# Index scores of a sparse-attention layer: two of eight heads weighted and summed on TensorE with diagonal matrices

## The reference, cut to what matters

```python
sc = jnp.einsum('bqhd,bsd->bqhs', qi, ki).astype(jnp.float32)              # 8 heads, 32 wide
idx_score = jnp.einsum('bqhs,bqh->bqs', jax.nn.relu(sc), wi.astype(jnp.float32))
idx_score = jnp.where(chunk_mask(q_pos, k_pos)[None], idx_score, -jnp.inf)
_, sel = lax.top_k(idx_score, topk)
```

## Time and profile before

| | |
|---|---|
| median of 3 runs | 3009.12 us (3008.86 to 3010.0) |
| the profiled execution, own time | 3013.24 us |
| its span, first to last instruction | 3011.5 us |
| mean granted TensorE clock over the span | 0.962 of full speed |
| busy: PE, DVE, ACT, POOL | 93%, 67%, 47%, 18% of the span |
| the index-score stage | 229.8 to 291.2 us, 61.4 us, 2% of the span |

### The profile page before, as it was taken

One profiled execution on the slowest core, in us unless ns is written; L12 is line 12 of the kernel. 1 busy time (PEld: TensorE's weight loads), 2 busy tenths in 40 slices (PEclk: granted clock), 3 DMA queues, 4 the chain that ended last, 5 costly groups with the idle time before them and its releaser, 6 DMA issues. The chain is left out here.

```text
span 3011.5 us, 49026 instructions
## 1 busy us (share of the span) xinstructions
PE 2801.6 (93%) x18237; PEld 2366.5 (79%) x18237; DVE 2022.9 (67%) x3648; ACT 1413.7 (47%) x2850; POOL 536.1 (18%) x410
## 2 busy tenths in 40 slices
PE   8986997999899999899899799999898999998998
PEld 6762564668899999778799567865688999998887
DVE  5447999865767776787631665139757777677777
ACT  5335996552444344433243455348724444444333
POOL 0000222420001110465000231000000111114641
PEclk9995999999999999999999799999999999999999
DMA  4111001022223332653411201120212333326432
GB/s 154 46 36 29 14 14 50 2 65 74 68 93 108 107 100 93 238 170 128 169 50 53 85 2 53 56 77 2 65 67 61 100 107 101 102 92 226 155 129 103
DMA packets 203118, 259.01 MB, mean 86 GB/s; under 512 B 27100, under 2 KB 132180, under 8 KB 202900
## 3 DMA queue, kind: packets, MB, share of 16 engines
q1 hardware_dynamic: 202900, 256.10, 25.9%
HBM read 177.90 MB, written 77.64 MB: 85 GB/s over the span
## 5 line engine op out<-in xcount | busy, mean ns | idle before, releaser
L247 PE MATMUL X<-up_th,high 128*128 128x272 f32 x1232 | 358.8, 291 | 12.4 <-DVE mixed_a_r L2377 4.8
L249 PE MATMUL X<-up_th,low_r 128*128 128x272 f32 x1232 | 357.4, 290 | 0.0
L247 PEld LDWEIGHTS X<-up_th,high 128*128 128x128 f32 x1232 | 234.7, 190 | 16.2 <-ACT up_U L2260 5.7
L2221 POOL TENSOR_TENSOR up_sum<-up_U 128x512 f32<-128x512 f32 x20 | 33.4, 1670 | 1136.8 <-DVE up_U L2372 1136.8
L249 PEld LDWEIGHTS X<-up_th,low_r 128*128 128x128 f32 x1232 | 234.3, 190 | 0.0
L2354 DVE SCALAR_TENSOR_TENSOR up_cv<-up_G,tap,up_cv 128x1024 f32<-128x1024 f32 (+1 forms) x176 | 130.3, 782 | 136.8 <-ACT up_cv L2269 135.3
L247 PE MATMUL up_x<-up_th,up_high 128*128 128x272 f32 x704 | 202.9, 288 | 1.4 <-DVE up_low_r L1835 1.4
L249 PE MATMUL up_x<-up_th,up_low_r 128*128 128x272 f32 x704 | 203.7, 289 | 0.0
L248 PE MATMUL X<-sums_r,high 128*128 128x272 f32 x528 | 152.0, 288 | 0.0
L247 PE MATMUL up_y<-up_th,up_high 128*128 128x272 f32 x528 | 151.9, 288 | 0.0
L249 PE MATMUL up_y<-up_th,up_low_r 128*128 128x272 f32 x528 | 151.5, 287 | 0.0
(11 more groups left out here) (553 smaller groups left out, 8606.4 us busy)
## 6 DMA issues: line engine op xcount, KB each, us to landing
scratch_a<-up_U SPq DMA_DIRECT2D x44, 544.0 KB, 2.7
low<-in_w_up_dram SPq DMA_DIRECT2D x44, 512.0 KB, 5.0
up_low<-in_w_up_dram SPq DMA_DIRECT2D x44, 512.0 KB, 4.7
scratch_s<-up_sum SPq DMA_DIRECT2D x80, 256.0 KB, 2.0
b_f<-in_w_down_dram SPq DMA_DIRECT2D x40, 512.0 KB, 4.5
a_lo_p_f<-scratch_s SPq DMA_DIRECT2D x40, 512.0 KB, 4.1
a_lo_p_f<-scratch_a SPq DMA_DIRECT2D x30, 512.0 KB, 4.4
scratch_att<-out_x SPq DMA_DIRECT2D x16, 512.0 KB, 2.6
```

The lines of the kernel that those rows point to most:

```text
L247: nc.tensor.matmul(out, lh, rh, start=first, stop=False, skip_group_check=on_top)
L249: return nc.tensor.matmul(out, ll, rh, start=False, stop=last, skip_group_check=on_top)
L2221: g.tensor_tensor(t0, a21, a22, ALU.add).then_inc(pair_summed, 1)
```

## The change

Each chunk becomes three units in place of two: heads 0 and 1, heads 2 to 4, heads 5 to 7. There are 33 units, still two buffers of each kind, now three heads large (`S`, three banks each; `relu`). Units alternate between the two buffers, u % 2.

The two heads of a chunk's first unit are no longer weighted by DVE. POOL makes, for each of the seven query tiles, two diagonal matrices `diag[q, h, q] = wi[q, h]` (the identity times a column of `wi`, two TENSOR_SCALARs of 128 x 128), in two buffers by tile. PE multiplies each relu result by its diagonal matrix, and the two matmuls add up in a PSUM bank `total[x % 2]` (`weighted`). DVE's first operation of a chunk takes that bank as its addend, so DVE has six SCALAR_TENSOR_TENSORs for a chunk and no TENSOR_SCALAR.

PE's order is, for each chunk x: scores of unit 0, scores of unit 1, `weighted(x)`, scores of unit 2. `weighted(x)` waits for the relu of unit 0, for the tile's diagonals and for the bank. ACT's relu of a unit waits for the reader of the unit two before it: PE's `total_done` where that was a chunk's first unit, DVE's `acc_done` where it was the second or third. POOL builds the first tile's diagonals ahead of the memsets of `bias`. The stage has seven semaphores in place of four.

```diff
--- before.py
+++ after.py
@@ -1557,17 +1557,22 @@
         sb, sem = ph.sb, ph.sem
 
         work = src["work"]
-        relu = [sb(f"relu{s}", [P, 4, 512]) for s in range(2)]
-        S = [ph.ps(f"s{s}", (P, 2048)) for s in range(2)]
+        relu = [sb(f"relu{s}", [P, 3, 512]) for s in range(2)]
+        diag = [sb(f"diag{s}", [P, 2, P]) for s in range(2)]
+        S = [ph.ps(f"s{s}", (P, 3 * 512)) for s in range(2)]
+        total = [ph.ps(f"total{s}") for s in range(2)]
         s_ready, relu_done, acc_done = sem("s_ready"), sem("relu_done"), sem("acc_done")
+        diag_done, total_done, ident_read = sem("diag_done"), sem("total_done"), sem("ident_read")
         set_up = sem("set_up")
         block = ph.block()
         qiT, kiT, wi, bias, at, top = (src[x] for x in ("qiT", "kiT", "wi", "bias", "bias_at", "top"))
         order = [NT] + SEARCHED
-        units = [(t, c0, min(512, key_tile(t)[0] - c0), c) for t in order for c0 in range(0, key_tile(t)[0], 512) for c in range(2)]
-
-        def heads(s, n, cw):
-            return S[s][:].rearrange("p (r c) -> p r c", r=4)[0:n, :, 0:cw]
+        heads_of = ((0, 1), (2, 3, 4), (5, 6, 7))
+        chunks = [(j, t, c0, min(512, key_tile(t)[0] - c0)) for j, t in enumerate(order) for c0 in range(0, key_tile(t)[0], 512)]
+        last_chunk = [max(x for x, c in enumerate(chunks) if c[0] == j) for j in range(len(order))]
+
+        def scored(u, n, cw):
+            return S[u % 2][:].rearrange("p (r c) -> p r c", r=3)[0:n, 0:len(heads_of[u % 3]), 0:cw]
 
         @block.sync
         def _(sp):
@@ -1577,36 +1582,68 @@
 
         @block.tensor
         def _(pe):
-            for u, (t, c0, cw, c) in enumerate(units):
-                k0 = key_tile(t)[1] + c0
-                n = queries(t)
+            def scores(x, part):
+                j, t, c0, cw = chunks[x]
+                u, k0, n = 3 * x + part, key_tile(t)[1] + c0, queries(t)
                 if u >= 2:
                     pe.wait_ge(relu_done, FROM + u - 1)
-                for r in range(4):
-                    hp = slice(32 * r, 32 * r + 32)
-                    last = nc.tensor.matmul(heads(u % 2, n, cw)[:, r, :], qiT[hp, c, t * P:t * P + n], kiT[hp, k0:k0 + cw],
+                for r, h in enumerate(heads_of[part]):
+                    hp = slice(32 * (h % 4), 32 * (h % 4) + 32)
+                    last = nc.tensor.matmul(scored(u, n, cw)[:, r, :], qiT[hp, h // 4, t * P:t * P + n], kiT[hp, k0:k0 + cw],
                                             start=True, stop=True)
                 last.then_inc(s_ready, 1)
+
+            def weighted(x):
+                j, t, c0, cw = chunks[x]
+                n = queries(t)
+                pe.wait_ge(relu_done, FROM + 3 * x + 1)
+                pe.wait_ge(diag_done, FROM + 2 * j + 2)
+                if x >= 2:
+                    pe.wait_ge(acc_done, FROM + 6 * (x - 2) + 1)
+                for r in range(2):
+                    last = nc.tensor.matmul(total[x % 2][0:n, 0:cw], diag[j % 2][0:n, r, 0:n], relu[3 * x % 2][0:n, r, 0:cw],
+                                            start=r == 0, stop=r == 1)
+                last.then_inc(total_done, 1)
+
+            for x in range(len(chunks)):
+                scores(x, 0)
+                scores(x, 1)
+                weighted(x)
+                scores(x, 2)
 
         @block.gpsimd
         def _(pool):
             g = nc.gpsimd
-            g.memset(bias[:, at[0]:at[2]], 0.0).then_inc(set_up, 1)
-            pool.wait_ge(set_up, FROM + 1)
-            for t in range(2):
-                b1 = at[t] + key_tile(t)[0]
-                g.memset(bias[0:P // 2, b1 - P // 2:b1], NEG).then_inc(set_up, 1)
-            pool.wait_ge(set_up, FROM + 3)
-            g.memset(bias[DEC:P, at[NT]:at[NT] + key_tile(NT)[0]], 0.0)
+            for j, t in enumerate(order):
+                n = queries(t)
+                if j >= 2:
+                    pool.wait_ge(total_done, FROM + last_chunk[j - 2] + 1)
+                for h in range(2):
+                    g.tensor_scalar(diag[j % 2][0:n, h, 0:n], consts["ident"][0:n, 0:n], wi[0:n, t, h:h + 1], 1.0,
+                                    ALU.mult, ALU.mult).then_inc(diag_done, 1)
+                if j == 0:
+                    pool.wait_ge(diag_done, FROM + 2)
+                    g.memset(bias[:, at[0]:at[2]], 0.0).then_inc(set_up, 1)
+                    pool.wait_ge(set_up, FROM + 1)
+                    for i in range(2):
+                        b1 = at[i] + key_tile(i)[0]
+                        g.memset(bias[0:P // 2, b1 - P // 2:b1], NEG).then_inc(set_up, 1)
+                    pool.wait_ge(set_up, FROM + 3)
+                    g.memset(bias[DEC:P, at[NT]:at[NT] + key_tile(NT)[0]], 0.0).then_inc(set_up, 1)
+                    pool.wait_ge(set_up, FROM + 4)
 
         @block.scalar
         def _(act):
-            for u, (t, c0, cw, c) in enumerate(units):
-                n = queries(t)
-                act.wait_ge(s_ready, FROM + u + 1)
-                if u >= 2:
-                    act.wait_ge(acc_done, FROM + 4 * (u - 1))
-                nc.scalar.activation(relu[u % 2][0:n, :, 0:cw], heads(u % 2, n, cw), ACT.Relu).then_inc(relu_done, 1)
+            for x, (j, t, c0, cw) in enumerate(chunks):
+                for part in range(3):
+                    u, n = 3 * x + part, queries(t)
+                    act.wait_ge(s_ready, FROM + u + 1)
+                    if u >= 2:
+                        if (u - 2) % 3 == 0:
+                            act.wait_ge(total_done, FROM + (u - 2) // 3 + 1)
+                        else:
+                            act.wait_ge(acc_done, FROM + 6 * ((u - 2) // 3) + 3 * ((u - 2) % 3))
+                    nc.scalar.activation(relu[u % 2][0:n, 0:len(heads_of[part]), 0:cw], scored(u, n, cw), ACT.Relu).then_inc(relu_done, 1)
 
         @block.vector
         def _(dve):
@@ -1616,21 +1653,25 @@
                 w = key_tile(t)[0]
                 v.memset(top["over"][:, j:j + 1], float(w - TOPK_P))
                 v.memset(top["limit"][:, j:j + 1], float(w - TOPK_P if j < BY_DVE else w + 1 - 2 * TOPK_P))
-            for u, (t, c0, cw, c) in enumerate(units):
+            for x, (j, t, c0, cw) in enumerate(chunks):
                 n = queries(t)
                 wk = work[t][0:n, c0:c0 + cw]
-                dve.wait_ge(relu_done, FROM + u + 1)
-                for r in range(4):
-                    f = wi[0:n, t, 4 * c + r:4 * c + r + 1]
-                    if c == 0 and r == 0:
-                        v.tensor_scalar(wk, relu[u % 2][0:n, r, 0:cw], f, None, ALU.mult).then_inc(acc_done, 1)
-                    else:
-                        dve.wait_ge(acc_done, FROM + 4 * u + r)
-                        v.scalar_tensor_tensor(wk, relu[u % 2][0:n, r, 0:cw], f, wk, ALU.mult, ALU.add).then_inc(acc_done, 1)
+                for part in (1, 2):
+                    u = 3 * x + part
+                    dve.wait_ge(relu_done, FROM + u + 1)
+                    for r, h in enumerate(heads_of[part]):
+                        f, z = wi[0:n, t, h:h + 1], relu[u % 2][0:n, r, 0:cw]
+                        if part == 1 and r == 0:
+                            dve.wait_ge(total_done, FROM + x + 1)
+                            so_far = total[x % 2][0:n, 0:cw]
+                        else:
+                            dve.wait_ge(acc_done, FROM + 6 * x + 3 * (part - 1) + r)
+                            so_far = wk
+                        v.scalar_tensor_tensor(wk, z, f, so_far, ALU.mult, ALU.add).then_inc(acc_done, 1)
                 w = key_tile(t)[0]
-                if c == 0 or c0 + cw < w:
+                if c0 + cw < w:
                     continue
-                dve.wait_ge(acc_done, FROM + 4 * u + 4)
+                dve.wait_ge(acc_done, FROM + 6 * x + 6)
                 if t < NT:
                     v.memset(work[t][0:P // 2, w - P // 2:w], -3.0e38)
 
```

## The result

The changed kernel takes 3028.14 us (median of 4 runs, 3025.61 to 3034.29), the kernel before beside it 3009.56 (4 runs): ratio 1.0058, 95% interval 1.0045 to 1.0071, or 13.5 to 21.4 us more. The forecast was 3020.7 in a range of 3012 to 3030, with 0.77 on slower. The profiled execution took 3025.61 us against 3013.24 for that of before, 12.4 more.

What follows compares the result with a forecast made beforehand. DVE was taken to bound the index stage before the change. Terms: 7.0 us slower at full clock plus 18.4 / 3 for half clock, 13.1, less 1.5 in the next stage, 11.6; median 3009.1 to 3020.7, range 3012 to 3030.

Steps and rivals of the forecast that it cites:

- The bound and DVE's work: Index stage: DVE sets the end; its operations per chunk fall from eight to six, ridding it of 12.5 us.
- The start: Index stage's beginning: DVE's first weighting operation waits for POOL's diagonals and PE's product, 5.7 us late at 238.4.
- The serial step: Each chunk but the first: the second unit's relu runs in DVE's idle time, 13.8 us together.
- Rival 3: Index stage: no serial step, DVE bounds, 6.8 us faster, 3002; chance 0.03.
- The clock: PE in the index stage: clock changes back and forth; 7.0 us slower at full clock, 25.4 at half, 13.1 expected.
- a third of the chunks at half clock: PE in the index stage: expected share at half clock, adding 18.4 / 3 to 7.0, making 13.1 us.
- the new stage at half clock leaves PE no break, so the clock rises: PE in the index stage: unbroken work at half clock would raise the clock; no separate size.
- Rival 2: Index stage: half clock throughout or costly shape switches, PE bounds every chunk, +25 us, 3034; chance 0.12.
- Switching shapes: PE around each product: going between 32 and 128 rows, 22 times each way, costs from nothing to 8.4 us.
- The next stage: Start of the stage after index: PE's clock may still be up, giving back 0 to 3.0 us, 1.5 taken.
- The sum: Whole kernel: 13.1 - 1.5 = 11.6 us slower; profiled execution 3024.8, median 3020.7.

Runs made afterwards that it cites:

- The clearing run: Changed kernel, with SP and not POOL clearing the previous stage's semaphores at the start of the index stage: 3023.26 us, ratio 1.0045.
- The three buffers: Changed kernel with three relu buffers in place of two, one for each unit of a chunk: 3017.71 us, ratio 1.0029.
- the split alone: Kernel before, with units of two, three and three heads and two buffers, DVE weighting all eight heads: 3015.11 us, ratio 1.0013.
- The thin fillers: Changed kernel plus three unused 384-column products on 32 rows of PE before the first product with the diagonals: 3027.43 us, ratio 1.0056.
- the full fillers: Changed kernel plus three unused 384-column products on 128 rows of PE before the first product with the diagonals: 3022.89 us, ratio 1.0044.
- the run with fillers and the late product: Changed kernel, three relu buffers, product last, DVE weighting the first and last two chunks wholly, unused PE products in those four: 3020.06 us, ratio 1.0030.
- the late product: Changed kernel with three relu buffers, the product after unit 2's scores, and DVE weighting the first two chunks wholly: 3016.29 us, ratio 1.0011.
- the repeat: The changed kernel itself, unaltered, profiled and timed again: 3027.19 us, ratio 1.0056 against the kernel before.

## Why the prediction was right, and where not

**The bound and DVE's work.** As predicted: 66 operations, 752 ns with both operands in SBUF and 747 with the addend in PSUM, no penalty as the earlier trace rows had it. The busy time of the weighting operations in the stage falls from 54.0 to 42.7 us, and none of it reaches the end.

**The start.** Predicted 238.4 for DVE's first operation, measured 239.11 in a stage that began 0.5 later; POOL's diagonals were expected from 235.2 and came at 235.89. The term, 5.7 us, measured 5.8 against the stage's start (8.5 for 2.7). The clearing run shows the mechanism.

**The serial step.** Predicted 1.45 + 0.15 = 1.60 us for a 512-wide chunk and a pitch of 6.3; measured 1.58 and 6.33. The three buffers show that it is this buffer, and the split alone shows that DVE's first two operations of a chunk had covered most of the relu. Rival 3, that DVE would stay the bound, was wrong for the reason given.

**The clock.** The size was right by luck: a third of the chunks at half clock was a guess, and the path to it was not the one that the trace shows. Predicted: 7.0 us with the clock up and 6.1 for a third of the chunks at half, 13.1; measured 13.6, of which 7 are the terms above. Nearly all of the other 6.6 lies in two places: the gap before the second chunk, 4.8 us where the serial step accounts for 1.6, and those of the last chunk, 3.6 (with a MEMSET in it) and 0.8 where it accounts for 1.3. But the step "the new stage at half clock leaves PE no break, so the clock rises" failed: PE had no break from 236.6 to 247.8, busy 11.16 us, and the clock rose only at the end of that. What was expected in its place, a clock that changes back and forth in the middle, did not come either: it held for 44.3 us with PE busy 77%, and fell once, in the narrow chunk. The thin fillers and the split alone show the missing term: units of two and three heads are on 64 or 96 of 128 rows, and in the split PE worked on them for 13.65 us without a break and stayed at half clock. Rival 2 had it as a remark ("fill less of the array") where it belonged in the sum.

By the Trainium skill ("TensorE: Matmul & The Clock Gate", section "Why this matters for your kernels") only longer gaps bring a raised clock down. The trace agrees for the 44.3 us in the middle, but at 292.1 the clock fell with no gap on PE over 1.26 us, PE busy 1.55 of 3.40 us. The same section of the Trainium skill says to keep TensorE busy without a break to get the full clock. Here that held for the full fillers on 128 rows; with the thin fillers, with the split alone, and with the mixture in the run with fillers and the late product, it did not.

**Switching shapes.** Predicted between nothing and 8.4 us. At full clock four MATMULs of a product stream for 4 x 0.427 = 1.71 us, and the next scores start 258.93 - 257.01 = 1.92 us behind the first, 0.2 us more. Half of that lies between the product's first MATMUL and its second, as it does inside a unit of scores too; the other 0.1 is the way back to 32 rows. The way in shows the same 0.1: the last MATMULs of the unit at 250.36 start at 250.78, stream 384 columns for 0.32 us, and the product starts at 251.21. Where unit follows unit with no switch (269.15 and 269.58 in the late product, 512 columns) there is no such 0.1. So both switches cost 0.2 us, 2.2 for eleven products, mostly hidden. By the Trainium skill ("TensorEngine Tiling (Array Packing)", section "Tiling Modes") a change of mode drains the engine; if this is that drain, it is small.

**The next stage.** Predicted 1.5 us back. It spends 3.8 us at half clock (305.4 to 309.2) before its first rise where it spent 6.0, which at half the speed is 1.1 saved. But that does not last: from its first MATMUL to that of attention A it takes 219.3 us, and 218.6 in the repeat, where it took 218.6. So of the 1.5 nothing is seen at the end of the stage.

**The sum.** The stage began 0.5 us later and took 13.6 more, and attention B took 0.7 more, so attention A begins 14.8 us later. Between the two profiled executions there are 12.4 us: the rest of the program took 2.4 us less, with nothing changed in it. That the 12.4 stands so near the forecast's 11.6 is therefore in part chance. The forecast missed the median by 7.4 us, and only 0.8 of it is in this difference. It also took the profiled execution to lie 4.1 us above the median, as before the change; afterwards it lay 2.5 below. The medians differ by 18.6 us in the first comparison and by 15.7 in the repeat (3027.19 for 3011.45), with intervals of 13.5 to 21.4 and 13 to 21. The 2 to 5 us beyond the stage's 13.6 have no cause on record. Time outside the stage scatters by 9 us over the profiled executions, and the granted clock in attention B and A falls at other places in each of them, which would do it, but that is argued and not shown.

## What to carry to other kernels

When work is taken from the engine that bounds, ask what that engine's work was covering: here the two heads taken from DVE had hidden the relu of the next unit, and an odd number of units over two buffers turned that relu into a step that no other work overlaps. Look at what the new helper's queue is doing when its first result is needed; POOL was still clearing the semaphores of the stage before. And before giving TensorE work on the strength of its idle time, cost it at the clock that it has in that stage: matmuls that use only some of the array's rows left it at half clock here though it was busy for 13 us without a break.

## What was not expected of the hardware

- PE busy for 20.9 us without a break, at half clock throughout, on matmuls of two or three groups of 32 rows with 128-row ones between them. In the kernel before, the clock rose some 3 us into an unbroken stretch of units on all four groups.
- PE busy for 13.65 us without a break on units of two and three heads, at half clock throughout, in the run with the split only.
- Two fillings of the same 4 us, equal in length and count, 128 rows and 32 rows: clock up before 236.4 in the one, not before 246.6 in the other, and 6.9 us between the stages.
- The clock pattern of this stage came out the same in two executions of the changed kernel (at half until 247.8 and from 292.1 in the one, until 248.1 and from 292.5 in the other) although the times of the runs go from 3025.6 to 3034.3 us; the slower executions were not profiled.
